# Eight modulation units moved from the first mixer's passes to the end of the mixture behind the convolution, in three slots apart from the overflow's

## The reference, cut to what matters

```
mod = jax.nn.silu(c) @ w_mod[i] + b_mod[i]                  # first block
mod = (cs @ ada_w[i] + ada_b[i])[:, None, :]                # second and third, w: 1024 x 6144
sh1, sc1, gt1, sh2, sc2, gt2 = jnp.split(mod, 6, axis=-1)
h = rmsnorm(x, norm_w[i, 0]) * (1.0 + sc1) + sh1            # ... mixer, x = x + gt1 * rmsnorm(y)
h = rmsnorm(x, norm_w[i, 2]) * (1.0 + sc2) + sh2            # ... mixture, x = x + gt2 * rmsnorm(y)
```

## Time and profile before

| | us |
|---|---|
| median of 3 runs | 2630.17 (2624.46 to 2630.81) |
| the profiled execution's own time | 2629.60 |
| its span, first to last instruction | 2627.8 |
| first mixer's passes in it | 155.5 to 493.7 |
| mixture behind the convolution | about 1005 to 1585.6 |

### The profile page before, as it was taken

How to read it: one execution, slowest core, us unless ns; L and a number is a source line. 1 busy time by engine, 2 the same in 40 slices (tenths; PEclk the granted TensorE clock), 3 DMA queues, 4 the chain that set the end, 5 groups by cost and what they waited for, 6 DMA issues and landing times. The chain is left out here.

```text
span 2627.8 us, 43428 instructions
## 1 busy us (share of the span) xinstructions
PE 2165.7 (82%) x18238; PEld 1520.7 (58%) x18238; DVE 1246.3 (47%) x1974; ACT 775.6 (30%) x1303; POOL 209.4 (8%) x204
## 2 busy tenths in 40 slices
PE   5999999896974899887778766899998897768766
PEld 3977777794542789543334335677777643334433
DVE  3367676644323444543333335666555643334334
ACT  4266666431112423311111114444423411111112
POOL 2000000101101000000000002111111000000001
PEclk8999999896997899899889887999999999989988
DMA  9157675428997322899999982211113699999995
GB/s 354 45 192 245 221 242 187 127 97 336 385 421 291 108 96 113 337 397 417 419 419 415 415 355 82 65 50 50 43 49 137 243 366 416 419 418 414 412 416 210
DMA packets 211851, 684.69 MB, mean 261 GB/s; under 512 B 23022, under 2 KB 122039, under 8 KB 152503
## 3 DMA queue, kind: packets, MB, share of 16 engines
q1 hardware_dynamic: 198742, 646.01, 64.0%
q0 software_dynamic: 8912, 21.04, 2.3%
q10 hardware_dynamic: 3984, 14.68, 1.4%
HBM read 671.68 MB, written 21.00 MB: 264 GB/s over the span
## 5 line engine op out<-in xcount | busy, mean ns | idle before, releaser
L221 PE MATMUL PS<-second 128*128 128x256 f32 (+1 forms) x4944 | 931.0, 346 | 54.0 <-DVE second L251 21.8
L221 PEld LDWEIGHTS PS<-second 128*128 128x128 f32 x4944 | 760.9, 193 | 200.6 <-DVE second L251 29.1
L221 PE MATMUL PS<-ring,arena 128*32 128x256 f32 (+5 forms) x6288 | 667.6, 456 | 212.5 <-DMA ring<-in_moe_w_down 67.0
L221 PEld LDWEIGHTS PS<-ring,arena 128*32 128x32 f32 (+2 forms) x6288 | 316.9, 125 | 450.0 <-issue 309.4
L221 PE MATMUL PS<-arena 128*32 128x256 f32 (+10 forms) x2480 | 499.6, 383 | 77.0 <-DMA ring<-in_moe_w_up 22.2
L221 PEld LDWEIGHTS PS<-arena 128*32 128x32 f32 (+4 forms) x2480 | 248.2, 151 | 242.4 <-issue 172.8
L233 ACT ACTIVATE arena<-PS 128x512 f32<-128x512 f32 (+1 forms) x217 | 106.1, 489 | 589.4 <-PE PS L221 504.5
L240 DVE TENSOR_TENSOR arena<-PS,arena 128x512 f32<-128x512 f32 (+1 forms) x305 | 210.6, 690 | 100.4 <-PE PS L221 73.5
L240 DVE TENSOR_TENSOR arena<-arena,PS 128x256 f32<-128x256 f32 (+1 forms) x77 | 41.0, 532 | 411.0 <-PE PS L221 409.9
L233 ACT ACTIVATE arena<-arena 128x128 f32<-128x128 f32 (+4 forms) x299 | 176.1, 589 | 201.4 <-DVE arena L240 69.6
L240 DVE TENSOR_TENSOR second<-ring,second 128x1024 fp32r<-128x1024 f32 (+1 forms) x90 | 149.0, 1656 | 157.5 <-ACT second L233 151.7
(11 more groups left out here) (166 smaller groups left out, 1380.8 us busy)
## 6 DMA issues: line engine op xcount, KB each, us to landing
ring<-in_moe_w_down SPq DMA_DIRECT2D x124, 1024.0 KB, 16.3
ring<-in_moe_w_up SPq DMA_DIRECT2D x121, 1024.0 KB, 15.4
ring<-in_moe_w_gate SPq DMA_DIRECT2D x109, 1024.0 KB, 16.5
ring<-in_ada_w SPq DMA_DIRECT2D x48, 1024.0 KB, 5.4
arena<-in_moe_w_gate SPq DMA_DIRECT2D x28, 1024.0 KB, 11.7
ring<-in_w_mod SPq DMA_DIRECT2D x22, 1024.0 KB, 7.0
arena<-in_moe_w_up SPq DMA_DIRECT2D x19, 1024.0 KB, 14.8
spare<-in_moe_w_gate SPq DMA_DIRECT2D x17, 1024.0 KB, 15.7
```

The source lines that it names most:

```text
L221: return P.e.matmul(o, l, r, start=st, stop=sp)
```

## The change

Units 13 and 14 are issued ahead of pass 0 with unit 12. The passes hold units 15 to 63, four in most, two in passes 0, 3, 4, 8 and 9. The units' loads take three slots by turns (0, `SPARE`, 4). Units 64 to 71 are computed at the end of the mixture behind the convolution, before the transposes of x, in PSUM banks 5 and 6 and with a copy of the conditioning that GpSimd makes there; SyncE loads them into slots 17, 18 and `SPARE`, after the overflow's loads. The overflow, of all three mixtures, now takes the eight ring slots 0 to 7 in turn, from slot 0. Groups 16 and 17 are turned and added in the gated delta rule's first steps, the last mixture's scale and shift go through memory there, and the router's preparation moves from steps 4 and 5 to the last two of twelve.

```diff
+    LATE = 16
+    crep_late = view(28928, 8, 32)
+    mrows_late = [view(29952 + 256 * i, 256) for i in range(2)]
     def mod_pe(n):
-        which = MODS[n // 24][1]
         w, g, r = unit("mod", n, k=2), n // 4, n % 4
-        b = PS[:, 3, 0:256]
-        P.wait_ge(at("ld", "mod", n), at("crep"), at("ev", "mod", g - 1) if r == 0 and g else None)
+        late = g >= LATE
+        rep_ = crep_late if late else crep[MODS[n // 24][1]]
+        if late:
+            b = take(state["late"], "modb", g, done=("ev", "mod", g)) if r == 0 else bank("modb", g)
+        else:
+            b = PS[:, 3, :]
+            P.wait_ge(at("ev", "mod", g - 1) if r == 0 and g else None)
+        P.wait_ge(at("ld", "mod", n), at("crep late") if late else at("crep"))
...
     MODS_OF = [[] for _ in range(16)]
-    for n in range(13, 72):
-        MODS_OF[(n - 13) // 4].append(n)
+    n = 15
+    for it, places in enumerate(("23", "0123", "0123", "01", "23", "0123", "0123", "0123", "01", "23", "0123", "0123", "0123", "0123", "012")):
+        MODS_OF[it] = [n + places.index(q) if q in places else None for q in "0123"]
+        n += len(places)
+    ENDS = [next((n // 4 for n in ms if n and n % 4 == 3), None) for ms in MODS_OF]
...
         half_sp(1, 0, ("ps", "v", 2, 2))
+        turn = slots(0, SPARE, 4)
+        state["slots"][4] = ("ps", "v", 3, 2)
+        for n in range(12, 15):
+            mod_sp(n, turn)
         ahead_sp(0)
-        turn = slots(0, 4)
-        state["slots"][4] = ("ps", "v", 3, 2)
         ahead_sp(1)
-        mod_sp(12, turn)
...
-        mods_pe((12,))
+        mods_pe((12, 13, 14))
...
-        overflow(m, S, count, lambda n: moe_load_more(m, turn, n, count), *(state["ring"][i] for i in (*range(8), SPARE, 20, *((8, 11, 13) if m.shared else ()))))
+        more = slots(*range(8))
+        overflow(m, S, count, lambda n: moe_load_more(m, more, n, count), *(state["ring"][i] for i in (*range(8), *((8, 11, 13) if m.shared else ()))))
...
         elif m.shared:
+            if m.i == 1:
+                turn = slots(17, 18, SPARE)
+                for n in range(4 * LATE, 72):
+                    mod_sp(n, turn)
             S.wait_ge(at("ps", "cm", m.i, m.NB - 1, 3, 1))
...
             if m.i == 1:
                 again_ac(name, t)
+                if t > 1:
+                    mod_ac(4 * (LATE + t - 1) - 1)
...
             fill(RTY[:, 0:1], 0.0, "passed", m.i)
+            if m.i == 1:
+                G.wait_ge(at("ps", "cm", m.i, m.NB - 1, 0, 0))
+                fill(crep_late, 0.0)
+                gcp(crep_late[:, :, 0], sc[:, 16:24], "crep late")
...
     def gates_first_pe():
         turn = state["all"]
+        state["late"] = banks(5, 6)
+        for n in range(4 * LATE, 72):
+            mod_pe(n)
         transposed2_pe(XN, "hG", turn, "m1")
...
         tr(b[:, 0:128], baT).then_inc(*P.mark("ps", "bat"))
+        for g in range(LATE, 18):
+            mod_turn_pe(g, turn)
         yield
         yield
-        prep_pe(MO[2])
         b = take(turn, "gc")
...
+        yield from steps(8)
+        prep_pe(MO[2])
         yield
...
-        prep_ve(MO[2], 0)
+        for g in range(LATE, 18):
+            mod_ve(g)
+        mods_used_ve(1, 1, "gts late")
         yield
...
-        prep_ve(MO[2], 1)
         V.wait_ge(at("egc"))
         tt(egP, egP, beP, ALU.mult)
+        yield from steps(6)
+        prep_ve(MO[2], 0)
+        yield
+        prep_ve(MO[2], 1)
...
     def gates_gp():
         G.end("gdn")
         meet(G, "gdn")
+        G.wait_ge(at("gts late"))
+        mixed_gp({2: abn[1][1]}, "ab_d late", "abp late")
```

More of the change, by code:

```diff
@@ L454, in mod_ac @@
         if n % 4 == 3:
-            A.wait_ge(at("ps", "mod", n), at("ps", "modt", g - 2) if g > 1 else None)
-            act(mrows[g % 2], PS[:, 3, 0:256], ACT.Copy, "ev", "mod", g)
+            late = g >= LATE
+            A.wait_ge(at("ps", "mod", n), at("ps", "modt", g - 2) if 1 < g < LATE else None)
+            act(mod_rows(g), bank("modb", g)[:, 0:256] if late else PS[:, 3, 0:256], ACT.Copy, "ev", "mod", g)
     def mod_ve(g):
@@ L724, in hgrn_sp @@
             for n in MODS_OF[it]:
-                mod_sp(n, turn)
+                if n:
+                    mod_sp(n, turn)
             if it < 12:
@@ L800, in mods_pe @@
         for n in ns:
-            mod_pe(n)
-            if n > 12 and n % 4 == 0:
+            if n:
+                mod_pe(n)
+            if n and n > 12 and n % 4 == 0:
                 mod_turn_pe(n // 4 - 1, state["body"])
@@ L818, in hgrn_pe @@
             if it == 15:
-                mod_turn_pe(17, state["body"])
-                state["banks"][3] = ("ev", "mod", 17)
+                mod_turn_pe(15, state["body"])
+                state["banks"][3] = ("ev", "mod", 15)
                 state["all"] = banks(*ALL)
@@ L922, in hgrn_ac @@
             if it == 14:
-                state["pairs"]["turn"] = Turn((1, 0), {0: ("ps", "mod", 71), 1: ("ps", "z", 15)})
+                state["pairs"]["turn"] = Turn((1, 0), {0: ("ps", "mod", 63), 1: ("ps", "z", 15)})
                 high(("ps", "g", 0, 1), "g", 0)
-            if MODS_OF[it]:
-                mod_ac(MODS_OF[it][2])
+            if ENDS[it]:
+                mod_ac(4 * ENDS[it] + 3)
             if it < 13:
@@ L1035, in hgrn_ve @@
             turned_ve(it)
-            if 1 <= it < 15:
-                mod_ve(it + 2)
+            if 1 <= it < 15 and ENDS[it - 1]:
+                mod_ve(ENDS[it - 1])
             scores_ve(it)
@@ L1206, in gate_ve @@
         meet(V, "hgrn")
[L1207 to L1210, removed]
+        for i, s in ((0, 0), (0, 1), (1, 0)):
+            mods_used_ve(i, s, "gts")
         V.wait_ge(at("hs"), at("ld", "rows"))
@@ L1275, in gate_gp, with mixed_gp @@
         G.wait_ge(G.here())
-        for i, a in enumerate((ABS1[:, 32:48], abn[0][1], abn[1][1])):
+        mixed_gp({0: ABS1[:, 32:48], 1: abn[0][1]}, "ab_d", "abp")
+    def mixed_gp(mods, out_, in_):
+        for i, a in mods.items():
             G.e.dma_start(ab_d[i].rearrange("s (k p) -> p s k", p=128), a.rearrange("p (s k) -> p s k", k=8),
[L1278 to L1282, removed]
+                          allow_slow_non_contiguous=True).then_inc(*D("ab_d").next(out_))
+        G.wait_ge(at(out_))
+        for i in mods:
+            G.e.dma_start(abm[i].rearrange("p (s k) -> p s k", k=8), ab_d[i].rearrange("s (p k) -> p s k", p=128),
+                          allow_slow_non_contiguous=True).then_inc(*D("abp").next("ld", in_))
     XN, H2T = view(4096, 4, F), view(8192, 8, 512)
@@ L2222, in moe_ac @@
     def moe_ac(m):
-        A.wait_ge(at("ld", "abp"))
+        A.wait_ge(at("ld", "abp late" if m.i == 2 else "abp"))
         if m.i == 0:
```

19 lines of the change are left out of this document (11 added, 8 removed).

## The result

| | us |
|---|---|
| kernel before, median of 6 runs | 2629.94 (2624.46 to 2630.81) |
| changed kernel, median of 6 runs | 2640.34 (2634.31 to 2643.07) |
| ratio, with its 95% interval | 1.004 (1.003 to 1.0051) |
| changed kernel's profiled execution, and its span | 2634.31, 2632.1 |

The change makes the kernel slower, by 10 us or 0.4%. I had said 2632.5 with a range to 2640. The profiled execution of the changed kernel is the shortest of its six, so both kernels were profiled a second time. Instructions that all four executions share were matched, and the table gives by how much each stage is longer than in the first profile of the kernel before. (The times in its first column are that profile's.)

What follows compares the result with a forecast made beforehand. Most of the first mixer's passes were taken as bound by VectorE's elementwise chain, not TensorE. Passes -5.2, tail +8.1 and the rest 0 gave +2.9 us on the profiled 2629.60: 2632.5 us, range 2624 to 2640.

Steps and rivals of the forecast that it cites:

- the chain of loads at the mixture's end: Mixture behind the convolution: units 67 to 71 wait for loads, each usable 5.3 us after issue; transposes start at 1604.5.
- The passes: First mixer's sixteen passes: fewer units there win 5.2 us, between 1 and 10.1.
- the first steps: Gated delta rule's first units: moved router preparation and new small operations together 0, between -1.5 and +2 us.
- Pass 9: First mixer: without positions 0 and 1 and the turn before it, its scores don't wait for ScalarE; 5.1 us won.
- passes 3 to 5: First mixer: 1.7 us won, less 1.6 for half clock after a 4.2 us idle stretch before pass 5's scores; 0.1 left.
- Rival B: The passes are bound by TensorE after all: 10.1 us less there, tail as forecast, 2628 us; chance 0.13.
- The tail: End of the mixture behind the convolution: eight late units and their loads make it 8.1 us later, between 5.5 and 12.
- Rival A: The tail's idle TensorE time hides the units: delay of 1 to 2 us, passes give 8 to 10, 2622 us; chance 0.12.
- ScalarE's extra copies: Mixture's tail: these copies stand between tile squares and cost nothing; only 0.6 us for a bank still to be copied.
- The slots of the overflow: Last mixture: its first down load must wait for the unit before; cost 0, with a cover of 5.7 us.
- Rival D: The overflow's loads or the scale and shift's trip through memory are late: 2 to 5 us on top, 2636; chance 0.05.
- Rival C: TensorE at 1.2 GHz through the tail, and idleness before scores costs 1.6 us in two more passes: +8.5, 2638; chance 0.15.

Runs made afterwards that it cites:

- e3: The changed kernel with eight slots for the late loads, so that none waits for a unit: 2632.75 us, ratio 1.0018 to the kernel before.
- e4: The changed kernel, where SyncE issues the late loads only after VectorE's first addition behind the branch: 2635.63 us, ratio 1.0025 to the kernel before.
- e5b: The changed kernel with eight slots for the late loads and ScalarE's two copies one tile earlier: 2630.43 us, ratio 0.9999 to the kernel before.
- e1: The kernel before with the overflow's new slots alone (ring slots 0 to 7 in turn): 2626.94 us, ratio 0.9999.
- e8b: The kernel before with the router's preparation in the last two of the twelve first steps: 2627.42 us, ratio 0.9991.
- e2: The changed kernel without the late loads and six of the eight late units; 2609.91 us, no measure, as the last mixture then has no overflow unit.
- e7b: The kernel before with two of pass 14's unit loads issued ahead of the last product's weights: 2625.09 us, ratio 0.9984.
- e11: The kernel before with pass 14's new load order and the late router preparation, no unit moved: 2623.34 us, ratio 0.9981.
- e6b: e5b with all three unit loads of pass 14 ahead of the load of the last product's weights: 2621.97 us, ratio 0.9971 to the kernel before.

## Why the prediction was wrong, point by point

Two steps failed most. The sum has no term for the stretch from the last unit's matmuls to the combination, and it grew by 2 to 3 us, as VectorE's branch was held up by the loads in flight. And the chain of loads at the mixture's end was reckoned with 5.3 us a load, which is the shortest of the earlier trace rows; it was 7.2 in the median. The passes came 1.5 us too good besides, and the first steps 2.5 too dear.

**The passes: right in kind, 1.5 us too good.** I had -5.2. Five executions with the changed passes (after twice, e3, e4, e5b) are 4.1 us shorter there in the mean, four with the old ones (before twice, e1, e8b) 0.4: a gain of 3.7. Pass 9 gave 5.0 of the forecast 5.1, and pass 1 nothing, by the half clock and ScalarE's copy as the steps had it (its scores wait 2.48 us, where I had 3.0). The miss is in passes 3 to 5: I had 0.1 us won, with 1.6 us for the half clock after the wait, and the five executions lose 0.9 in the mean, as the half clock lasts longer in three of them. Pass 15, behind the wait in pass 14 that stayed, begins at half clock in some executions and not in others. Rival B falls.

**The tail: the mechanism right, 1 to 2 us too cheap.** I had +8.1; the two profiles show +9.3 and +9.8. The load chain was as written: units 64 to 66 ran at 2.4 GHz (32 instructions in 1.93 us), the loads waited for units to end, and 67 began 6.4 us after the combination, as forecast. From there each step was longer. The load of unit 70 went out at 1590.59 and was used at 1597.91, 7.3 us instead of the 5.3 that I took from the earlier trace rows. That row has 5.3 as its shortest and 8.5 as its median, and I took the shortest. The eight late loads took 5.3, 7.2 and 8.7 us (shortest, median, longest), and the DMA engines were 96% busy in this stretch (the row at the end of this section). So from the combination's end to the transposes it was 21.5 us (1582.17 to 1603.71) against my 18.9. The transposes then took 4.30 us where I had 5.7 (5.19 in the second profile). My remark that a load of 4.4 us would take 1.3 us off the sum is wrong as well: it enters in two rounds, so it would be 1.8. The sum doesn't use it. Rival A falls, and "the loads can't keep up" was only half of why: e3_eight gave the loads all the slots they could use and still cost 4.5. **The sentence that holds only by accident is "ScalarE's extra copies stand between tile squares and are hidden".** They are hidden under the load chain and nowhere else; in the changed kernel the last one costs 0.50 us, near the 0.6 that I had. I had noted that the transposes take all eight banks, and priced that as a copy, instead of asking where in ScalarE's queue the copy stands.

**The missing term: +2.8 us for the branch.** I went from the end of the last unit to the combination as if nothing in it could change, though the row of the wait names its releaser, `DVEq L58`. With the loads in flight TensorE's wait is 7.73, 6.79, 7.82 and 8.03 us (after twice, e3, e5b); without, 4.47, 4.20, 4.20 and 4.20 (before twice, e2, e4). The stretch itself is 3.3 and 2.3 us longer in the two profiles. No rival had it. That the fetch of the branch's target goes through the same DMA engines as the loads is what the instruction packets in the queue tables suggest; the experiments show that the loads are the cause, not the way in which they are. The Trainium skill, "Runtime: NRT & Kernel Launch", section "Instruction fetch mechanics", says that a taken branch whose target isn't in the prefetched window has to fetch it by DMA before the engine can go on; the 3 us of idleness in the quiet case agree with that, and the page has no number for either case.

**The first steps: -2.5 us, not 0.** I let the wait of 2.86 us be replaced by others and forgot that the sixteen matmuls (3.57 us, 2.01 at their new place) stood on the path too, while at their new place they wait 0.23 us behind 24 us of products. My range of -1.5 to +2 missed it. e8b shows it alone, with 4.1.

**The slots of the overflow: 0, right.** Rival D falls, with e1 and with the copy at 1656.23 that didn't wait.

**The sum.** By these terms: -3.7 + 2.8 + 9.5 - 2.5 = +6 us, where I had +2.9. The ratio says 8 to 13. The rest lies in the other stages, as far as the profiles can tell. Take the mean of each stage over the six profiles with the old passes (before twice, e1, e7b, e8b, e11) and the seven with the changed ones (after twice, e2 up to 1573, e3, e4, e5b, e6b). The changed ones are 1.1 us shorter ahead of the passes, 2.7 longer from 482.0 to 1573.0 and 0.6 longer from 1631.0 to the end, and 0.4 us more of the time lies outside the span. With these the sum is 8 to 9. But these stages scatter by up to 5 us between executions, so neither the 2.7 nor its cause is shown. In single kernels the four stages do better: for e5b_early_copy, -3.7 for the passes and the other three stages of its own profile add up to 0.3 us and it measured 0.9999; for e4_wait they give +6.3, and it measured 1.0025, which is 6.6; for e3_eight +1.6, at the lower end of its interval (1.3 to 8.2 us). So whether the changed kernel has a hidden term, and of what size, stays open. Rival C came nearest in size (2638), from the wrong place: its point of decision was a clock of 0.50 past 1604. TensorE's granted clock from unit 67 to the transposes was 0.50, but it was 0.76 from 1604 to 1606 and 1.00 after, the 32 transposes took 4.30 us, and the passes kept most of their gain.

```profile
1588.60:1603.70 15.10, 9.67 (x80) 2.97 (x80) 7.15 (x7) 5.08 (x14) 2.50 (x1) 0.50 0.96 320
```

(Columns as in the earlier trace rows.)

## What to carry to other kernels

The idle stretch here took in the moved work, all but 1.5 us, only when its loads no longer waited for one another's slots and nothing that runs in the stretch waited for the moved work's last result; go through every queue, and through every engine's place in it, for both. A wait that ends with a sequencer's line is a branch or a meeting: note it as a cost, and ask what else uses the DMA engines in those microseconds before starting loads there. And do the small edits at each place first: here the order of three loads and the place of sixteen matmuls were worth some 5 us (1.6 to 8), the move of eight units nothing even with its tail mended. And where a row gives a shortest, a median and a longest time of a load, don't build a chain on the shortest.

## What the runs showed of the hardware

VectorE's taken branch over the overflow unit costs 2.8 to 3.1 us with quiet DMA queues, in eight executions, and 5.4 to 6.6 us with 1 MB loads in flight (96 to 100% of the DMA engines' time), in five (after twice, e3, e5b, e6b). It is seen in no engine's busy time, only as a wait of others for a `DVEq` line. A late eviction can cost more than itself: where eight banks are taken at once, the last copy of 0.38 us held 32 transposes for 3.3 us (e3_eight). And the price of a stop of TensorE isn't fixed: behind the same wait of 4.1 us before pass 5 the half clock cost up to 1.6 us more in some executions than in others.
